# Weight tiles kept in a partition-major bf16 copy in DRAM after the first token tile (hybrid attention and state-space layer, 8 cores)

## The reference

```python
h = rms_norm(x, norm1_g)
proj = h @ w_in                     # q | k | v | u | gates   (1024 x 3328)
attn_out = sliding_window_attention(rope(q), rope(k), v)     # window 128, per-head sinks
ssm_out  = s5_branch(u)                                       # diagonal state-space scan + GLU
merged = sigmoid(g1) * (attn_out @ w_branch_attn) + sigmoid(g2) * (ssm_out @ w_branch_ssm)
x = x + merged @ w_out
h2 = rms_norm(x, norm2_g)
x = x + (silu(h2 @ w_ffn_gate) * (h2 @ w_ffn_up)) @ w_ffn_down   # d_ff = 2816
y = rms_norm(x, norm_f_g)
```

## Time and profile before

| what | us |
| --- | --- |
| median of 2 runs | 1851.26 (1848.56 to 1853.96) |
| the profiled execution, its own time | 1851.81 |
| its span on core 1, the slowest | 1850.3 |
| spans of the eight cores | 1821.2 to 1850.3 |
| busy on core 1: TensorE, VectorE, ScalarE, GpSimd | 1340.6, 776.5, 467.2, 103.9 |

### The profile page before, as it was taken

One profiled execution on the slowest core, in us unless ns is written; L12 is line 12 of the kernel. 1 busy time (PEld: TensorE's weight loads), 2 busy tenths in 40 slices (PEclk: granted clock), 3 DMA queues, 4 the chain that ended last, 5 costly groups with the idle time before them and its releaser, 6 DMA issues.

```text
span 1850.3 us, 28712 instructions; the slowest of 8 cores (1821.2 to 1850.3 us)
## 1 busy us (share of the span) xinstructions
PE 1340.6 (72%) x9222; PEld 697.8 (38%) x9222; DVE 776.5 (42%) x1900; ACT 467.2 (25%) x826; POOL 103.9 (6%) x126
## 2 busy tenths in 40 slices
PE   0032778798878277876899576899489689986995
PEld 0032446386666122332344222344233233433431
DVE  0667266675566154462113462213363221243223
ACT  0021523424322362431110532210342221013101
POOL 0000000000000000000011000011100000100110
PEclk9996766666765578878999778999766799998998
DMA  7001311210000675524779806789901549995881
GB/s 129 0 1 33 110 45 49 69 47 24 3 2 2 137 142 85 75 46 69 114 114 156 197 5 110 102 121 141 219 5 19 82 78 138 127 185 95 130 130 47
DMA packets 130500, 156.62 MB, mean 85 GB/s; under 512 B 9392, under 2 KB 119632, under 8 KB 130320
## 3 DMA queue, kind: packets, MB, share of 16 engines
q0 software_dynamic: 114112, 106.96, 40.3%
q1 hardware_dynamic: 16240, 47.82, 8.1%
HBM read 252.85 MB, written 10.96 MB: 143 GB/s over the span
## 4 chain that ended last, share of the span: by engine, by line
PE 51%; DMA 22%; DVE 13%; issue 9%; ACT 4%; SPq 1%; DVEq 0%; ACTq 0%; POOLq 0%
PE ps L1066 9%; DMA arena<-w_fu 7%; PE ps L1050 5%; PE ps L1052 5%; DMA arena<-xo 4%; PE ps L712 4%; PE ps L663 4%; DVE arena L451 3%; PE ps L1013 3%; PE pt L593 2%; PE ps L1034 2%; PE ps L1011 2%; DMA arena<-w_ba 2%; DMA arena<-w_fd 2%; DMA arena<-w_bs 2%
## 5 line engine op out<-in xcount | busy, mean ns | idle before, releaser
L1052 PE MATMUL ps<-arena 128*128 128x512 bf16 (+1 forms) x880 | 263.2, 345 | 24.8 <-DMA arena<-w_fu 23.8
L1050 PE MATMUL ps<-arena 128*128 128x512 bf16 (+1 forms) x880 | 261.8, 341 | 4.8 <-ACT arena L1054 4.4
L593 PE MATMUL pt<-identb,arena 128*128 128x128 bf16 (+1 forms) x536 | 102.8, 269 | 150.8 <-DVE arena L589 64.2
L1055 DVE TENSOR_TENSOR arena<-ps,arena 128x512 bf16<-128x512 f32 x110 | 64.7, 588 | 288.7 <-PE ps L1050 165.3
L1066 PE MATMUL ps<-arena 128*128 128x512 bf16 (+1 forms) x748 | 175.3, 387 | 13.7 <-DMA arena<-w_fd 13.7
L1052 PEld LDWEIGHTS ps<-arena 128*128 128x128 bf16 x880 | 80.1, 99 | 125.5 <-issue 39.1
L1013 PE MATMUL ps<-arena 128*128 128x512 bf16 (+1 forms) x320 | 108.1, 382 | 26.3 <-DMA arena<-w_in 25.1
L1054 ACT ACTIVATE arena<-ps 128x512 f32<-128x512 f32 x110 | 56.6, 515 | 278.9 <-PE ps L1050 225.1
L587 ACT ACTIVATE arena<-arena 128x1024 bf16<-128x1024 f32 (+1 forms) x67 | 70.6, 1053 | 208.3 <-DVE arena L1035 78.1
L593 PEld LDWEIGHTS pt<-identb,arena 128*128 128x128 bf16 (+1 forms) x536 | 53.0, 117 | 180.3 <-issue 169.3
L712 PE MATMUL ps<-arena 32*128 32x64 bf16 x2048 | 108.6, 282 | 11.6 <-DVE arena L736 3.5
(11 more groups left out here) (192 smaller groups left out, 1904.2 us busy)
## 6 DMA issues: line engine op xcount, KB each, us to landing
arena<-xo SPq DMA_DIRECT2D x48, 512.0 KB, 5.4
arena<-w_fg POOLq DMA_DIRECT2D x20, 1024.0 KB, 11.7
arena<-w_fu POOLq DMA_DIRECT2D x20, 1024.0 KB, 15.0
arena<-w_in POOLq DMA_DIRECT2D x17, 1024.0 KB, 16.8
arena<-w_fd POOLq DMA_DIRECT2D x16, 1024.0 KB, 14.9
arena<-xp SPq DMA_DIRECT2D x16, 512.0 KB, 3.9
arena<-w_out POOLq DMA_DIRECT2D x8, 1024.0 KB, 13.7
y<-arena SPq DMA_DIRECT2D x16, 512.0 KB, 5.0
```

Source lines behind the costliest of these rows:

```text
L593: op("pe", lambda e, kc=kc: e.transpose(out=pt[:, kc * 128:kc * 128 + rows], in_=tmp_bf[0:rows, kc * 128:(kc + 1) * 128], identity=identb[ ...
L1050: op("pe", lambda e, kc=kc, pg=pg, ff=ff, lc=lc, n=n, wg=wg: e.matmul(pg[:, 0:n], lhsT=wg[:, kc, ff * 128:(ff + 1) * 128], rhs=h2T[:, kc, ...
L1052: op("pe", lambda e, kc=kc, pu=pu, ff=ff, lc=lc, n=n, wu=wu: e.matmul(pu[:, 0:n], lhsT=wu[:, kc, ff * 128:(ff + 1) * 128], rhs=h2T[:, kc, ...
```

## The change

In tile 0 each ring slot is loaded as before, and then also written out by a DMA on SP to a DRAM tensor of its own, `[128, n]` in bf16, a row for each partition. In tiles 1 to 3 Pool loads the slot from this tensor, as it lies: one run of 8 KB for each partition (6 or 8 KB for w_fd, 4 KB for the last pair of w_fg and w_fu), no cast. The two branch weights of a half share a slot, and so in tiles 1 to 3 one DMA takes the place of two. The write reads the slot, so a slot's next load also waits for it; the later load reads the DRAM tensor and so waits for its write.

```diff
-            def wload(src_ap, nk, ncols):
+            SCR = {}
+            def scratch(key, n):
+                if key not in SCR:
+                    SCR[key] = (nc.dram_tensor("wscr_" + key, [128, n], BF16).ap(), TB(None))
+                return SCR[key]
+
+            def wload(src_ap, nk, ncols, key=None, ti=0):
...
+                scr, sb_ = scratch(key, nk * ncols)
+                if ti == 0:
+                    op("pool", lambda e: e.dma_start(out=view, in_=src_ap.rearrange("(k p) c -> p k c", p=128)), [], [slot], chan="wr%d" % i)
+                    op("sp", lambda e: e.dma_start(out=scr, in_=flat), [slot], [sb_], chan="ws%d" % i)
+                else:
+                    op("pool", lambda e: e.dma_start(out=flat, in_=scr), [sb_], [slot], chan="wr%d" % i)
...
+                    scr_b, sbb_ = scratch("br_%d" % dg, 4096)
+                    if ti == 0:
+                        op("pool", lambda e, vba=vba, dg=dg: e.dma_start(out=vba, in_=w_ba[:, dg * 512:(dg + 1) * 512].rearrange("(k p) c -> p k c", p=128)), [], [slot], chan="wr%d" % i_)
...
+                        op("sp", lambda e, slot=slot, scr_b=scr_b: e.dma_start(out=scr_b, in_=slot[:, 0:4096]), [slot], [sbb_], chan="ws%d" % i_)
+                    else:
+                        op("pool", lambda e, slot=slot, scr_b=scr_b: e.dma_start(out=slot[:, 0:4096], in_=scr_b), [sbb_], [slot], chan="wr%d" % i_)
```

More of the change, by code:

```diff
@@ L598, in body @@
             wr_i = {"i": 0}
-            def wload(src_ap, nk, ncols):
+            SCR = {}
[4 more added lines that the diff above has]
+            def wload(src_ap, nk, ncols, key=None, ti=0):
                 wr_i["i"] = (wr_i["i"] + 1) % 4
                 slot = WRING[wr_i["i"]]
-                view = slot[:, 0:nk * ncols].rearrange("p (k c) -> p k c", c=ncols)
+                flat = slot[:, 0:nk * ncols]
+                view = flat.rearrange("p (k c) -> p k c", c=ncols)
                 i = wr_i["i"]
-                op("pool", lambda e: e.dma_start(out=view, in_=src_ap.rearrange("(k p) c -> p k c", p=128)), [], [slot], chan="wr%d" % i)
+                if key is None:
+                    op("pool", lambda e: e.dma_start(out=view, in_=src_ap.rearrange("(k p) c -> p k c", p=128)), [], [slot], chan="wr%d" % i)
+                    return TB(view, slot.b)
+                scr, sb_ = scratch(key, nk * ncols)
+                if ti == 0:
+                    op("pool", lambda e: e.dma_start(out=view, in_=src_ap.rearrange("(k p) c -> p k c", p=128)), [], [slot], chan="wr%d" % i)
+                    op("sp", lambda e: e.dma_start(out=scr, in_=flat), [slot], [sb_], chan="ws%d" % i)
+                else:
+                    op("pool", lambda e: e.dma_start(out=flat, in_=scr), [sb_], [slot], chan="wr%d" % i)
                 return TB(view, slot.b)
@@ L996, in tile_main @@
                 for dg in range(2):
-                    wg1 = wload(w_in[:, 1280 + dg * 512:1280 + (dg + 1) * 512], 8, 512)
-                    wg2 = wload(w_in[:, 2304 + dg * 512:2304 + (dg + 1) * 512], 8, 512)
+                    wg1 = wload(w_in[:, 1280 + dg * 512:1280 + (dg + 1) * 512], 8, 512, "g1_%d" % dg, ti)
+                    wg2 = wload(w_in[:, 2304 + dg * 512:2304 + (dg + 1) * 512], 8, 512, "g2_%d" % dg, ti)
                     wr_i["i"] = (wr_i["i"] + 1) % 4
@@ L1002, in tile_main @@
                     i_ = wr_i["i"]
-                    op("pool", lambda e, vba=vba, dg=dg: e.dma_start(out=vba, in_=w_ba[:, dg * 512:(dg + 1) * 512].rearrange("(k p) c -> p k c", p=128)), [], [slot], chan="wr%d" % i_)
-                    op("pool", lambda e, vbs=vbs, dg=dg: e.dma_start(out=vbs, in_=w_bs[:, dg * 512:(dg + 1) * 512].rearrange("(k p) c -> p k c", p=128)), [slot], [slot], chan="wr%d" % i_)
+                    scr_b, sbb_ = scratch("br_%d" % dg, 4096)
+                    if ti == 0:
+                        op("pool", lambda e, vba=vba, dg=dg: e.dma_start(out=vba, in_=w_ba[:, dg * 512:(dg + 1) * 512].rearrange("(k p) c -> p k c", p=128)), [], [slot], chan="wr%d" % i_)
+                        op("pool", lambda e, vbs=vbs, dg=dg: e.dma_start(out=vbs, in_=w_bs[:, dg * 512:(dg + 1) * 512].rearrange("(k p) c -> p k c", p=128)), [slot], [slot], chan="wr%d" % i_)
+                        op("sp", lambda e, slot=slot, scr_b=scr_b: e.dma_start(out=scr_b, in_=slot[:, 0:4096]), [slot], [sbb_], chan="ws%d" % i_)
+                    else:
+                        op("pool", lambda e, slot=slot, scr_b=scr_b: e.dma_start(out=slot[:, 0:4096], in_=scr_b), [sbb_], [slot], chan="wr%d" % i_)
                     wbr = TB(None, slot.b)
@@ L1027, in tile_main @@
                     load(TB(x1[0:rows, j, :], x1B[j]), src)
-                wo = [wload(w_out[:, hf_ * 512:(hf_ + 1) * 512], 8, 512) for hf_ in range(2)]
+                wo = [wload(w_out[:, hf_ * 512:(hf_ + 1) * 512], 8, 512, "wo_%d" % hf_, ti) for hf_ in range(2)]
                 for (g0, rows, j, ridx) in subs:
@@ L1042, in tile_main @@
                     nf = 4 if fg < 5 else 2
-                    wg = wload(w_fg[:, fg * 512:fg * 512 + nf * 128], 8, nf * 128)
-                    wu = wload(w_fu[:, fg * 512:fg * 512 + nf * 128], 8, nf * 128)
+                    wg = wload(w_fg[:, fg * 512:fg * 512 + nf * 128], 8, nf * 128, "fg_%d" % fg, ti)
+                    wu = wload(w_fu[:, fg * 512:fg * 512 + nf * 128], 8, nf * 128, "fu_%d" % fg, ti)
                     for ff in range(nf):
@@ L1059, in tile_main @@
                         nk = 8 if fgp < 2 else 6
-                        wd = wload(w_fd[fgp * 1024:fgp * 1024 + nk * 128, hf_ * 512:(hf_ + 1) * 512], nk, 512)
+                        wd = wload(w_fd[fgp * 1024:fgp * 1024 + nk * 128, hf_ * 512:(hf_ + 1) * 512], nk, 512, "fd_%d_%d" % (hf_, fgp), ti)
                         for si, (g0, rows, j, ridx) in enumerate(subs):
```

## The result

The changed kernel takes 1845.45 us in the median of 32 runs (1829.58 at the least) against 1855.73 for the kernel before in 31 runs beside them; the ratio is 0.9927, with a 95% interval of 0.9908 to 0.9946. The medians are of all runs, while the ratio is of those alone in which all eight cores ran in their faster state (23 of the 32), so it isn't the quotient of the two. The changed kernel is faster by 0.7%, some 14 us, where 2.6% (49 us) was forecast. The range that was given, 1766 to 1852, holds the median; the size of the step is off by more than three times.

A forecast was written before the change was run, and what follows sets the result against it. FFN stages were taken as bound by TensorE with DMA engines nearly full, other stages by single waits. Gains 62 + 8 + 18 = 88 and costs 33 + 6 = 39 gave -49 from 1851.8: 1802 us, range 1766 to 1852.

The forecast's parts named there:

- F2(0) moves by over 20: Tile 0's F2 stage: a stated sign that the prediction is wrong, if its time changes by more than 20 us.
- What a load costs: Weight loads from scratch: bytes read set the pace, so a slot occupies the engines 3.3 us in place of 6.7.
- Rival (a): Pool's queue itself is the slow part, so scratch loads are no quicker: 1879 us, slower; chance 0.10.
- The larger runs I cost at nothing: Scratch loads: runs of 8 KB in place of 2 KB were taken to bring no gain.
- Part 1: Tiles 1 to 3: 90% of TensorE's 69.3 us of waits for weight loads go, -62 us, bounds -40 and -69.
- Parts 2 and 3: Tiles 1 to 3: less low clock after waits, -8 us; quicker y stores and xo loads at tile starts, -18.
- Part 2: Tiles 1 to 3: less time at TensorE's lower clock after long waits, -8 us, bounds 0 and -13.
- rival (c): Other waits, psum evictions or norms, replace those removed, so half of the 88 us shows: 1847 us; chance 0.10.
- Part 4: FFN(0): writing out 17.3 MB makes the stage DMA-bound, +33 us, bounds +15 and +61.
- Part 5: F2(0) and B1(0): 8.4 MB of writes mostly hidden, SP stopping before the first, +6 us, bounds 0 and +20.
- Rival (b): Tile 0 gives most of the gain back, through slot waits and writes at their upper bound: 1834 us; chance 0.25.
- the ring's extra wait: FFN(0): a slot's next load waits for its write; costed at nothing, +25 us if not covered.

The follow-up runs named there:

- e3: Changed kernel with its bf16 copies kept in rows of 512 columns (256 for the last w_fg/w_fu pair), runs of 1 KB; ratio 0.9939 to the kernel before.
- e2: Changed kernel's writes alone: tiles 1 to 3 load float32 as before and the copies are never read; ratio 1.0407 to the kernel before.
- e7: As e2, but of each FFN slot in FFN(0) only the first half of the columns is written out; ratio 1.0289 to the kernel before.
- e1: Changed kernel with only SP's order changed: first four scratch writes issued behind the xo loads of F1(0) and F1(1); ratio 0.9809 to the kernel before.
- e4: Changed kernel without ring writes: Pool makes the copies DRAM to DRAM early, up to four at once, tile 0 loads them too; ratio 0.9677 to kernel before.
- e5: As e4, but 18 of 28 copies run in the preparation, three at a time, the other 10 singly; ratio 0.9542 to the kernel before.

## Why the prediction was wrong

It was wrong in size: -49 forecast, -14 measured. That the median lies in the stated range is no merit of the sum: the range was 86 us wide. Of its own signs of being wrong one came true, "F2(0) moves by over 20": stage A moved by 29. TensorE's waits for weight DMAs came to 73 us for "near 30". By its own parts (means of eight cores, from the table):

- *What a load costs.* Right that half the bytes read, without a cast, take about half as long and that Pool's queue is not slow by itself: 5.3 to 7.9 us for "5 to 7". Whether it is the bytes or the cast no run separates. Rival (a) fell by that row. "The larger runs I cost at nothing" was right for the time and wrong for the DMAs: e3's loads are 0.6 to 1.5 us longer and its writes 4 to 8.
- *Part 1, TensorE's waits in tiles 1 to 3*: -62 predicted, 69.3 less 12.5 is -57. FFN(1) ended at 120 for "near 118".
- *Parts 2 and 3*, the clock and the tile starts: -26 predicted. The gains are 86 in the mean against e2 (76 by the balance of the stages); less 57, that leaves 29 (19). Part 2 was too small rather than too large: TensorE's busy time in B, C and D fell by 20.5 us on core 1 for 8, though how much of it lay on the path no run shows. On core 1's chain the y stores and xo loads that stood for 61.0 us stand for 5.39 + 4.97 + 12.43 + 7.76 + 7.71 + 9.36 = 47.6, 13 less for 18. The rest was not taken apart; rival (c), other waits in their place, holds for a small part at most. Together the gains were 86 for 88.
- *Part 4, the writes in FFN(0)*: +33 predicted, +39 measured. The prediction had worked out 39 at the rate of a full share (285 GB/s read) and 19 with a better interleaving (318), and took 33; the better interleaving didn't come. In the changed kernel the stage moves 197 GB/s landed for 177 us, 34.9 MB, of which 17.3 are writes; the loads read twice what they land, save some 3 MB of copies for the next tile, so about 50 MB in 177 us, 280 GB/s by this estimate. e7 shows the excess to go with the bytes. That a slot's next load waits for its write was costed at nothing by the 14 us for which TensorE holds a pair of w_fg and w_fu; a w_fd slot is read for 7 us only, and there the wait stands in the chain once, for 11.78 us. What it adds to the stage wasn't measured apart.
- *Part 5, the writes in F2(0) and B1(0)*: +6 predicted with a bound of +20, **+29 measured in A alone, and 5 more in B by e2. This is the step that failed.** It had named the mechanism, "SP stops in front of the first write until its load lands, and xo loads are queued behind", and sized it by how busy the DMA engines are. What the 29 us came from is how long the first loads take to land, and who needs the xo load behind. The trace of before had both. Pool waits for w_ba to land, and xo loads fill the chain from 617 to 660 us:

```profile
667.07 0.76 POOL L1004 DMA_DIRECT2D arena<-w_bs  x1 [45.71 <-DMA arena<-w_ba]
```

```profile
617.85 7.15 DMA arena<-xo
...
627.45 18.30 DMA arena<-xo
...
649.63 10.43 DMA arena<-xo
```

The scheduler's estimate for w_ba, from which it chose where to put the writes, is 7.2 us (2.0 + 1.05 MB / 200 GB/s). A wait on an in-order queue is priced by the landing time of what is waited for, here 33 to 55 us from the start of the stage, and only then by what of it is hidden. e1 shows it by the one change of order: A goes from 130 to 101.

In the mean of the cores 49 was forecast and 9 came, 40 us apart. e2 splits them: the writes cost 77 for 39, of which Part 5 makes 28 and Part 4 6 of the excess, and the loads brought 86 for 88. (The ratio, of slowest cores, makes the 40 into 35.)

Rival (b), that tile 0 gives most back (1834, that is -18), came nearest to the change of -14, and its price of 70 nearly to the 77. It named "one SP queue in order" in its favour, but priced the ring's extra wait at +25 and the writes at their upper bound; what decided was the queue (e1) and the bytes (e7), so the closeness of the number is partly luck.

My expectations of e4 and e5 missed in the same way: work that is free on the engine that issues it was charged to the double-buffered loads beside it (e4) and to a fence that waits for all (e5).

## What to carry to other kernels

A write-back that "costs nothing" on an idle queue stops that queue until its source has landed: price it by the measured landing time, and look for what a fixed order has queued behind it, on the queue and on the engine that waits for that. Put copies for later reuse where the DMA engines have room, not where the data happens to be at hand. Here copies made in the first third of the kernel, from which tile 0 could load as well, brought 5.5%; made in tile 0, with its fullest stage, they brought 0.7%, or 1.9% with the queue's order mended. And before adding copies, look for loads that wait for each other without need: one such wait was worth 1.3%.

## What the runs showed of the hardware

- DMAs of Pool and SP together filled the engines to a share of 1.01 to 1.02 in FFN(0), with 280 GB/s read in the changed kernel and 293 in e2 (estimates, both from 197 GB/s landed). Loads alone read 285 at a full share; two queues brought hardly more than one.
- A packet loaded from float32 with a cast took 105 ns for 2 KB in and 1 KB out, which is the rate by bytes read of SP's loads without a cast (148 ns for 2.94 KB). From bf16 copies, half the bytes and no cast, 1 MiB landed in medians of 5.3 to 7.9 us (core 1), in runs of 1 KB in 6.4 to 8.3 (cores 1 and 7), where it was 11.7 to 16.8 before.
- Copies from DRAM to DRAM with a cast made a 512 KB load beside them take 11.3 us in place of 3.9 with up to four in flight (e4), and 6.3 with one at a time (e5).
